# Expert stage of a two-block transformer kernel: all of the last expert matrix in three products of rounded halves, one low half on GpSimd

## The reference, cut to what matters

```python
def body(acc, blk):
    tok, wt, e = blk
    xb = h[tok]
    hid = jax.nn.silu(xb @ w1[e]) * (xb @ w3[e])
    return acc.at[tok].add(wt[:, None] * (hid @ w2[e]).astype(f32)), None
```

## Time and profile before

| | |
|---|---|
| median of 3 runs | 2858.55 us (2857.12 to 2866.07) |
| the profiled execution: its own time | 2863.36 us |
| its span, first to last instruction | 2861.1 us |
| mean granted TensorE clock | 0.975 of full |
| busy over the span: TensorE, VectorE, ScalarE, GpSimd | 95%, 62%, 44%, 8% |
| moved by DMA | 442 MB, mean 155 GB/s |

### The profile page before, as it was taken

How to read it: one execution, slowest core, us unless ns; L and a number is a source line. 1 busy time by engine, 2 the same in 40 slices (tenths; PEclk the granted TensorE clock), 3 DMA queues, 4 the chain that set the end, 5 groups by cost and what they waited for, 6 DMA issues and landing times.

```text
span 2861.1 us, 42808 instructions
## 1 busy us (share of the span) xinstructions
PE 2706.0 (95%) x17240; PEld 2121.7 (74%) x17240; DVE 1779.2 (62%) x3174; ACT 1261.9 (44%) x2232; POOL 227.5 (8%) x212
## 2 busy tenths in 40 slices
PE   6998998889999999999978989999999998999998
PEld 6887777774777777777736766888888775888887
DVE  5257876676688888888745896432334688433333
ACT  3332554221277777777713337322223328422222
POOL 0000000000022222222200120000000030000000
PEclk9999997999999999999989999999999999999999
DMA  6210002424489999999874331314224340323321
GB/s 238 89 59 23 1 3 77 124 62 163 160 309 359 360 361 359 362 372 355 339 299 159 108 77 32 119 51 139 74 81 133 96 107 12 100 77 96 118 69 63
DMA packets 186546, 442.44 MB, mean 155 GB/s; under 512 B 21283, under 2 KB 110694, under 8 KB 167014
## 3 DMA queue, kind: packets, MB, share of 16 engines
q1 hardware_dynamic: 161862, 396.59, 38.6%
q0 software_dynamic: 24480, 43.04, 5.1%
HBM read 426.43 MB, written 38.29 MB: 162 GB/s over the span
## 4 chain that ended last, share of the span: by engine, by line
PE 78%; DVE 9%; DMA 6%; ACT 4%; issue 2%; SPq 0%; ACTq 0%; DVEq 0%; POOLq 0%
PE ps L296 19%; PE ps L298 19%; PE ps L297 19%; DMA ring<-in_ew 5%; PE ps L2534 3%; PE ps L2036 2%; PE ps L1519 2%; PE ps L2563 1%; PE ps L2781 1%; PE ps L2241 1%; DVE Pb L3530 1%; DMA yr<-y_rows 1%; DVE spA L2467 1%; DVE spB L2467 1%; PE ps L3419 1%
## 5 line engine op out<-in xcount | busy, mean ns | idle before, releaser
L2993 DVE TENSOR_TENSOR wf<-ring,wf 128x1024 fp32r<-128x1024 f32 (+1 forms) x152 | 181.7, 1196 | 312.3 <-ACT wf L2989 312.0
L2989 ACT ACTIVATE wf<-ring 128x1024 fp32r<-128x1024 f32 (+1 forms) x152 | 156.8, 1033 | 347.9 <-PE ps L298 347.9
L296 PE MATMUL ps<-hxh,wf 128*128 128x512 f32 (+1 forms) x736 | 279.9, 380 | 2.3 <-DVE hxl L3156 2.3
L297 PE MATMUL ps<-hxl,wf 128*128 128x512 f32 (+1 forms) x736 | 279.5, 380 | 0.0
L298 PE MATMUL ps<-hxh,wf 128*128 128x512 f32 (+1 forms) x736 | 279.5, 380 | 0.0
L2467 DVE TENSOR_TENSOR spA<-ring,spA 128x1024 fp32r<-128x1024 f32 x196 | 234.0, 1222 | 57.1 <-ACT spA L2462 56.3
L2462 ACT ACTIVATE spA<-ring 128x1024 fp32r<-128x1024 f32 x196 | 202.8, 1072 | 47.1 <-DMA ring<-in_ew 44.7
L296 PEld LDWEIGHTS ps<-hxh,wf 128*128 128x128 f32 x736 | 138.4, 188 | 28.9 <-DVE hxl L3156 2.7
L297 PEld LDWEIGHTS ps<-hxl,wf 128*128 128x128 f32 x736 | 138.4, 188 | 26.3
L298 PEld LDWEIGHTS ps<-hxh,wf 128*128 128x128 f32 x736 | 138.4, 188 | 25.9
L2467 DVE TENSOR_TENSOR spB<-ring,spB 128x1024 fp32r<-128x1024 f32 x129 | 157.2, 1219 | 0.4 <-ACT spB L2462 0.4
(11 more groups left out here) (630 smaller groups left out, 6555.0 us busy)
## 6 DMA issues: line engine op xcount, KB each, us to landing
ring<-in_ew SPq DMA_DIRECT2D x65, 2048.0 KB, 13.1
ring<-in_ew SPq DMA_DIRECT2D x65, 1024.0 KB, 7.7
ring<-in_w_in SPq DMA_DIRECT2D x17, 2048.0 KB, 8.7
ring<-in_w_gate SPq DMA_DIRECT2D x20, 1024.0 KB, 5.5
ring<-in_w_up SPq DMA_DIRECT2D x20, 1024.0 KB, 8.0
ring<-in_w_down SPq DMA_DIRECT2D x16, 1024.0 KB, 5.1
adaw<-in_ada_w SPq DMA_DIRECT2D x24, 512.0 KB, 6.3
ring<-in_w_out SPq DMA_DIRECT2D x6, 2048.0 KB, 8.5
```

The source lines that it names most:

```text
L296: pe.matmul(o, lhs[0], rhs[0], start=start, stop=False)
L297: pe.matmul(o, lhs[0], rhs[1], start=False, stop=False)
L2989: act.activation(item_part(n)[0], item_raw(n), ACT.Copy).then_inc(*w_hi.inc(n))
L2993: v.tensor_tensor(item_part(n)[1], item_raw(n), f(item_part(n)[0]), ALU.subtract).then_inc(*w_lo.inc(n))
```

## The change

Both halves of w2 go through `mm3`. The second half becomes piece 5: its high half `w5h` is made by ScalarE behind piece 4, its low half `w5l` by GpSimd (a new kind of step, 3, in `expert_pool`, between the scatter and the next gather). `hdT` isn't written in the experts' loop any more; what waited for it waits for `hdp` high. The room for `w5l` comes from `yb`, which has two buffers in place of three. TensorE's full-precision products of an expert are replaced by six rounded ones.

```diff
-    sb("gap", [128, D], c=b1)
+    w5h = sb("w5h", [128, D], R32, c=b1)
...
-    yb = sb("yb", [128, 3, D], c=m4)
+    yb = sb("yb", [128, 2, D], c=m4)
+    w5l = sb("w5l", [128, D], R32, c=m4)
...
+    p_lo5 = Signal(sem("gather_zero"), range(NX))
...
     def piece(e, j):
+        if j == 5:
+            return [w[:, :].rearrange("p (k n) -> p k n", k=2) for w in (w5h, w5l)]
...
     def pieces_act(act, e, js=range(4)):
...
+            elif j == 5:
+                if e:
+                    act.wait_ge(*k_pe.val(("y1", e - 1)))
...
     def expert_pool(g):
...
-        for k, n in [(0, 0)] + [(k, n + (k == 0)) for k, n in steps((0, 4))]:
-            if k == 0:
+        for k, n in [(0, 0)] + [(k, n + (k == 0)) for k, n in steps((0, 3, 4))]:
+            if k == 3:
+                g.wait_ge(*p_hi.val((n, 5)))
+                g.tensor_tensor(piece(n, 5)[1], piece_raw(n, 5), f(piece(n, 5)[0]), ALU.subtract).then_inc(*p_lo5.inc(n))
+            elif k == 0:
...
-                scatter(g, n, n % 3).then_inc(*d_sca.inc(n))
+                scatter(g, n, n % 2).then_inc(*d_sca.inc(n))
...
     def expert_pe(pe):
...
-                w2 = wv2[(n + 1) % 2].rearrange("p (k n) -> p k n", k=2)
-                pe.wait_ge(*wk2.val(n + 1))
...
-                pe.wait_ge(*p_lo.val((n, 4)))
-                for j in range(2):
-                    m = mm3(pe, ps[5][:, :], [hdp[:, q, j, :] for q in range(2)], [w[:, j, :] for w in piece(n, 4)], start=(j == 0), stop=(j == 1))
-                m.then_inc(*p_use.inc((n, 4)))
-                pe.wait_ge(*k_act.val(("hf", n)))
-                for j in range(2):
-                    m = pe.matmul(ps[6][:, :], hdT[:, j, :], w2[:, j, 512:1024], start=(j == 0), stop=(j == 1))
+                for q in range(2):
+                    pe.wait_ge(*(p_lo5.val(n) if q else p_lo.val((n, 4))))
+                    for j in range(2):
+                        m = mm3(pe, ps[5 + q][:, :], [hdp[:, x, j, :] for x in range(2)], [w[:, j, :] for w in piece(n, 4 + q)],
+                                start=(j == 0), stop=(j == 1))
+                    if q == 0:
+                        m.then_inc(*p_use.inc((n, 4)))
                 m.then_inc(*k_pe.inc(("y1", n)))
...
     def expert_act(act):
...
-                if n >= 3:
-                    act.wait_ge(*d_sca.val(n - 3))
-                act.activation(yb[:, n % 3, :].rearrange("p (q n) -> p q n", q=2), psa[:, 5:7, :], ACT.Copy).then_inc(*k_act.inc(("y", n)))
+                if n >= 2:
+                    act.wait_ge(*d_sca.val(n - 2))
+                act.activation(yb[:, n % 2, :].rearrange("p (q n) -> p q n", q=2), psa[:, 5:7, :], ACT.Copy).then_inc(*k_act.inc(("y", n)))
...
                 act.activation(hdp[:, 0, :, :], hT_, ACT.Copy).then_inc(*k_act.inc(("hd", n)))
-                act.activation(hdT[:, :, :], hT_, ACT.Copy).then_inc(*k_act.inc(("hf", n)))
-                pieces_act(act, n, (4,))
+                pieces_act(act, n, (4, 5))
...
     def expert_dve(v):
...
-                v.wait_ge(*k_act.val(("hf", n)))
+                v.wait_ge(*k_act.val(("hd", n)))
```

More of the change, by code:

```diff
@@ L2429, in _program @@
     k_pe = Signal(sem("expert_mm"), split_keys((1, 3, 4), {1: "t0 t1", 3: "hT", 4: "y1"}))
-    k_act = Signal(sem("expert_scalar"), split_keys((1, 2, 3, 4), {1: "t0 t1", 2: "silu", 3: "hd hf", 4: "y"}))
+    k_act = Signal(sem("expert_scalar"), split_keys((1, 2, 3, 4), {1: "t0 t1", 2: "silu", 3: "hd", 4: "y"}))
     k_dve = Signal(sem("expert_vector"), split_keys((1, 2, 3), {1: "t0 t1", 2: "hd2", 3: "hl"}))
@@ L2434, in _program @@
     g_hg = Signal(sem("gather_zero"), ["set"])
+    p_lo5 = Signal(sem("gather_zero"), range(NX))
     MADE = [(0, j) for j in range(4)] + [x for k, n in steps((2, 3)) for x in
-                                         ([(n, 4)] if k == 3 else [(n + 1, j) for j in range(4) if n + 1 < NX])]
+                                         ([(n, 4), (n, 5)] if k == 3 else [(n + 1, j) for j in range(4) if n + 1 < NX])]
     USED = [x for k, n in steps((2, 4)) for x in ([(n, 4)] if k == 4 else [(n, j) for j in range(4)])]
     p_hi = Signal(sem("piece_hi"), MADE)
-    p_lo = Signal(sem("piece_lo"), MADE)
+    p_lo = Signal(sem("piece_lo"), [x for x in MADE if x[1] < 5])
     p_use = Signal(sem("piece_mm"), USED)
     def piece(e, j):
+        if j == 5:
+            return [w[:, :].rearrange("p (k n) -> p k n", k=2) for w in (w5h, w5l)]
         m = 2 if j == 4 else 4 if j == 2 and e else j
@@ L2448, in piece_raw @@
     def piece_raw(e, j):
-        if j == 4:
-            return wv2[(e + 1) % 2].rearrange("p (k n) -> p k n", k=2)[:, :, 0:512]
+        if j >= 4:
+            return wv2[(e + 1) % 2].rearrange("p (k n) -> p k n", k=2)[:, :, 512 * (j - 4):512 * (j - 4) + 512]
         return wv13[(e + 1) % 2].rearrange("p (k n) -> p k n", k=8)[:, 2 * j:2 * j + 2, :]
@@ L2538, in expert_pe @@
                 if n:
-                    pe.wait_ge(*k_act.val(("hf", n - 1)))
+                    pe.wait_ge(*k_act.val(("hd", n - 1)))
                     pe.wait_ge(*k_dve.val(("hl", n - 1)))
@@ L2664, in over_pe @@
         pe.wait_ge(*k_dve.val(("hd2", NX - 1)))
-        pe.wait_ge(*k_act.val(("hf", NX - 1)))
+        pe.wait_ge(*k_act.val(("hd", NX - 1)))
         pe.wait_ge(*k_dve.val(("hl", NX - 1)))
```

## The result

The changed kernel takes 2867.44 us (median of 20 runs, 2864.16 to 2873.94), the kernel before 2861.91 us in the same comparison (20 runs, 2855.15 to 2866.07): ratio 1.0022, 95% interval 1.0015 to 1.0029. The prediction said 2854.5 in a range of 2838 to 2876. The time lies in the range, but it moved by +5.5 us, not by -4. The profiled execution's span is 2864.6 us.

A forecast was written before the change was run, and what follows sets the result against it. The weight queue, not TensorE, was taken to bind the expert stage (10.14 against 9.94 us per expert). Terms of -3 us in the stage and -1 us at the last expert gave -4: 2854.5 against 2858.55, range 2838 to 2876.

The forecast's parts named there:

- TensorE, -0.31 us per expert: Expert products: six rounded ones (1.41 us) replace two full-precision ones (1.72 us); -20 us for 65 if TensorE sets the pace.
- ScalarE, cost 0: Per expert, the full-precision hidden copy goes and a sixth conversion comes, +0.63 us, covered by the wait for the load.
- VectorE, "no work is added": Expert step: no added work; the hidden tile's low half starts 0.39 us earlier, T being the start of an output copy.
- the rival on VectorE: Expert steps: GpSimd's subtraction stalls VectorE's piece subtractions, which bind from 1.5 us; at 2.0 us, +31 us, 2890; chance 0.15.
- GpSimd, 2.0 us and hidden: New 1024-wide subtraction per expert, about T + 3.3 to T + 5.3, needed near T + 7.9; T starts an output copy.
- Gather, cost 0: Gather behind GpSimd's subtraction, issued at T + 5.7 instead of T + 3.35; taken as 0, at worst +12 us.
- Of 20 us only 3 reach the end, because the weight queue binds: Expert stage: same bytes, so only time in which DMA lacked work is won; -3 us, bounds 0 and -20.
- The 21.2 us between two loads into one buffer: Chain of waits from 1065.61 to 1086.82: read as 10.6 us per expert, 6.1 of them conversions.
- Sixty landings 10.14 us apart: Weight loads between 804.99 and 1410.81: 10.14 us per expert against TensorE's 9.94, read as the queue having fallen behind.
- Last expert, -1 us: Last expert, with no load to wait for: products end earlier or later, from -2.7 to +2 us, taken as -1.
- The gather comes late: Rival, gather behind GpSimd's subtraction: its landing moves in full, +12 - 4 us, 2867; chance 0.10.
- TensorE sets the pace: Rival, expert stage: DMA brings an expert in 9.63 us, so -20 - 1 us, 2837.5; chance 0.20.

## Why the prediction was wrong, step by step

**TensorE, -0.31 us per expert: right.** The undisturbed step went from 9.83 to 9.50 us (experiments without the low half), -0.33.

**ScalarE, cost 0: right.** +41.9 us of work (524.59 in the kernel without the low half against 482.69), 0.65 a step. It is in the kernel with fewer bytes and without the low half too, and there the steps are at TensorE's own 9.50 us.

**VectorE, "no work is added": this failed.** It was put at nothing in the sum; its instructions are the same, but 54 us longer. The step that failed stands in the rival on VectorE and is two sizes in one sentence. The overlap was put at 0.5 us, since at T + 3.3 to 5.3 VectorE mostly reads PSUM. It holds in some steps; the two `spA` subtractions behind it took 2.86 us at 972.47 and 3.38 at 993.38, +0.5 and +1.0. But in steps with row lists VectorE is late, and the subtraction of piece 4 stands for 2.05 us; the mean is 0.84. I had looked at one expert without a list. And the slack was put at 1.5 us, all of VectorE's idle time (97 / 64). After the change it was the bound and still idle for 43.3 us, 0.68 a step: in every step it waits for ScalarE's copies `hdp` and `spA` (13.8 and 15.0 us in the groups above), which come when the chain of the step brings them. Taken off, an estimate of 1.5 - 0.68 = 0.8 us of slack is left, and the stall was 0.84. (The 0.68 comes from the changed kernel itself, so the sum has to close; other kernels bound by VectorE were idle for less, 0.42 us a step with the low half on VectorE.)

A mean hides the rest. TensorE's own steps, as the kernel with fewer bytes and without the low half has them, are 9.50 us five times and 10.40 once, 57.9 us for six. The changed kernel needs 60.9, and 2.5 of the 3.0 us more stand in the two distances 9.97 and 11.54, at the step with the 3.27 us subtraction and behind it. The stalls of 0.5 us in the steps of 9.50 cost nothing. Three us in six steps make 32 us for 64, the 31.4 measured. A gain of 5 turned into a loss of 5.5.

**GpSimd, 2.0 us and hidden: size off, hidden right.** It takes 2.60 us on the mean and 2.41 undisturbed, within the bounds of 0.89 to 2.7. It started at T + 3.28 and ended at T + 5.69; TensorE never waits for it. The upper bound, both inputs in turn, was the better value.

**Gather, cost 0: right, its bound too high.** It is issued at T + 5.8. Its landing fell, as the DMA views of 804 to 1004 and 1044 to 1164 us show (median us to landing):

```profile
hg<-h_rows,idx POOLq DMA_INDIRECT x19, 6.8
...
ring<-in_ew SPq DMA_DIRECT2D x12, 2048.0 KB, 12.2
...
hg<-h_rows,idx POOLq DMA_INDIRECT x12, 7.7
```

From 15.4 to 7.7 us in the tight stretch, so it lands at T + 13.5 where it landed at T + 18.8: later issue, earlier landing. The weights came down too, from 14.5 to 12.2. Both fit a queue that is no longer behind, since VectorE, whose piece 3 the weights wait for, asks for them more slowly; in the kernel without the low half, where loads are late, the gather lands after 15.8 us in the same stretch. What share the later issue has in it wasn't measured. The bound of +12 compares with at most 5.7 us (the memsets).

**Of 20 us only 3 reach the end, because the weight queue binds: right in result once the stall is out.** Without the stall and the later gather 5 us arrived (0 to 8), the last expert's share among them, where -4 was the sum; with fewer bytes it was 27. But two of its reasons were wrong. The 21.2 us between two loads into one buffer come from the long steps, and its 6.1 us of conversions are of the 21.2, not of each 10.6. Sixty landings 10.14 us apart didn't show that the queue had been the pace before: 9.98 of that is TensorE's own mean step, lists included, and the loads cost the kernel before about 7 us in all, in its long steps (stage 643.4, with spread rows 636.5).

**Last expert, -1 us: right in this profile.** The last distance is 8.09 us, before 8.99. In the profiles of the experiments with the same products it lies between 8.26 and 9.62, so one profile doesn't settle a term of 1 us.

**The rivals.** "VectorE is held up by GpSimd" was the mechanism, given 0.15 and priced at 2890, with 2.0 us of stall in each step; 2867 came, from 0.84. The rule that the Trainium skill has for it ("SBUF — State Buffer", Who interferes with whom: a VectorE instruction with two SBUF inputs and a GpSimd one that reads SBUF exclude each other, whoever is first) agrees with the 3.27 us behind GpSimd's 2.41, and its limits with the memsets (1222 ns). "The gather comes late" named 2867 too, by accident: its mechanism isn't there, since TensorE waits for no gather. That the time lies inside the stated range is luck as well: the range reached up through that late gather and a part stall, and a part stall was in no term of the sum. "TensorE sets the pace" needed 2837; it holds only with fewer bytes (2834).

## What to carry to other kernels

Before GpSimd is given a two-input operation, look at every step of VectorE's pattern, the rare long ones first: where VectorE subtracts two SBUF tiles the two run in turn, and 2.6 us of "free" work can cost more than the 1.2 us that VectorE would need. Idle time of an engine is slack only as far as its inputs are there early; take off what it spends waiting for the step's own chain. Where gathered blocks are half full, look at which partitions they fill: that was worth 5 to 12 us here in kernels held up by their loads, for a reason that is still open. And compare busy time per step, not per window: a slower kernel has fewer steps in the same window.

## What the runs showed of the hardware that was not expected

- When VectorE and GpSimd both subtract two SBUF tiles, the row of the later one grows by what is left of the other's: VectorE's 512 columns 0.67 to 1.80 us, GpSimd's 1.40 to 2.34 us, VectorE's 1024 columns 1.22 to 3.27 us.
- Three memsets per expert on GpSimd (958 ns each) leave VectorE's two-input subtractions at 1222 ns, yet the wait for loads rose from 44.5 to 58.0 us.
- An indirect gather issued 2.5 us later landed 5 us earlier (from issue 7.7 us in place of 15.4), in a kernel whose loads were no longer late.
- Moving the same rows to other partitions, bytes unchanged, took 12 us from a kernel bound by its loads.
